# Ten projection tiles of the second block by seven products in place of eight

## The reference, cut to what matters

```python
h = rms_norm_2(x, g_pre) * (1 + scale) + shift
proj = h @ w_in                    # 1024 x 1024 by 1024 x 9216
q, k, v, g_att, u, g_lru, merge = jnp.split(proj, split_at, axis=-1)
y_a = (dilated_attention(q, k, v) * jax.nn.silu(g_att)) @ w_pa
u = causal_depthwise_conv(u, conv_w, conv_b)
y_b = (rg_lru(u, w_rg, b_rg, w_ig, b_ig, lru_lambda) * jax.nn.silu(g_lru)) @ w_pb
gate_a, gate_b = jnp.split(jax.nn.sigmoid(merge), N_BRANCHES, axis=-1)
out = (gate_a * y_a + gate_b * y_b) @ w_o
return x + gate * rms_norm_2(out, g_post)
```

## Time and profile before

| | us | share of span | instructions |
| --- | --- | --- | --- |
| median of the runs | 2834.89 | | |
| span of the profiled execution | 2834.6 | | 33566 |
| TensorE matmul (PE) | 2789.5 | 98% | 13780 |
| TensorE weight load (PEld) | 2343.3 | 83% | 13780 |
| VectorE (DVE) | 1838.1 | 65% | 2069 |
| ScalarE (ACT) | 1514.1 | 53% | 1619 |
| GpSimd (POOL) | 136.6 | 5% | 81 |

### The profile page before, as it was taken

The page is one execution under the profiler, slowest core; times in us unless marked ns, Lnnn a source line. Parts: engine busy times, 40 slices in busy tenths (PEclk is TensorE's granted clock), DMA queues, the critical chain, the costliest instruction groups (busy, mean ns, idle before and its releaser), DMA issues.

```text
span 2834.6 us, 33566 instructions
## 1 busy us (share of the span) xinstructions
PE 2789.5 (98%) x13780; PEld 2343.3 (83%) x13780; DVE 1838.1 (65%) x2069; ACT 1514.1 (53%) x1619; POOL 136.6 (5%) x81
## 2 busy tenths in 40 slices
PE   8999999879999999999999999999999999999999
PEld 7889988768888888888888878888888888888887
DVE  7564467778888888888888886333332256544344
ACT  5322322247777777777777776333333389743022
POOL 0211000110000000000000000000000011100000
PEclk9999999989999999999999999999999999999999
DMA  6222157789999999999999951110112211343332
GB/s 200 89 74 78 72 178 264 267 331 383 386 386 386 382 386 382 388 384 386 390 383 387 377 210 75 60 60 25 59 60 60 69 48 63 99 158 131 112 134 89
DMA packets 137273, 598.97 MB, mean 211 GB/s; under 512 B 17952, under 2 KB 39840, under 8 KB 80672
## 3 DMA queue, kind: packets, MB, share of 16 engines
q1 hardware_dynamic: 132224, 580.10, 54.7%
q0 software_dynamic: 4464, 16.25, 2.2%
q10 hardware_dynamic: 432, 0.47, 0.1%
HBM read 543.06 MB, written 52.53 MB: 210 GB/s over the span
## 4 chain that ended last, share of the span: by engine, by line
PE 97%; DVE 2%; ACT 0%; issue 0%; DMA 0%; SPq 0%; DVEq 0%; ACTq 0%
PE bank L442 26%; PE bank L444 25%; PE bank L443 25%; PE bank L1871 12%; PE bank L450 3%; PE bank L459 1%; PE bank L2444 1%; PE bank L1420 1%; PE bank L778 1%; PE bank L2817 0%; DVE r_sc L1654 0%; DVE r_at L1655 0%; DVE r_best L1651 0%; PE bank L2445 0%; PE bank L838 0%
## 5 line engine op out<-in xcount | busy, mean ns | idle before, releaser
L1819 DVE TENSOR_TENSOR e_wl<-e_raw,e_wh 128x2048 fp32r<-128x2048 f32 x381 | 870.8, 2291 | 123.9 <-ACT e_wh L1811 123.4
L1811 ACT ACTIVATE e_wh<-e_raw 128x2048 fp32r<-128x2048 f32 x384 | 735.6, 1919 | 184.6 <-PE bank L444 100.9
L442 PE MATMUL bank<-b_hid_h,b_wh 128*128 128x512 f32 x1148 | 452.1, 394 | 0.2
L444 PE MATMUL bank<-b_hid_h,b_wl 128*128 128x512 f32 x1148 | 447.4, 390 | 0.0
L443 PE MATMUL bank<-b_hid_l,b_wh 128*128 128x512 f32 x1148 | 446.9, 389 | 0.0
L442 PE MATMUL bank<-e_wh,e_xh 128*128 128x512 f32 x1020 | 403.4, 395 | 0.0
L444 PE MATMUL bank<-e_wh,e_xl 128*128 128x512 f32 x1020 | 398.1, 390 | 0.0
L443 PE MATMUL bank<-e_wl,e_xh 128*128 128x512 f32 x1020 | 396.9, 389 | 0.0
L442 PEld LDWEIGHTS bank<-b_hid_h,b_wh 128*128 128x128 f32 x1148 | 215.6, 188 | 46.5 <-issue 2.9
L444 PEld LDWEIGHTS bank<-b_hid_h,b_wl 128*128 128x128 f32 x1148 | 215.5, 188 | 45.6
L443 PEld LDWEIGHTS bank<-b_hid_l,b_wh 128*128 128x128 f32 x1148 | 215.7, 188 | 42.8
(11 more groups left out here) (508 smaller groups left out, 4354.8 us busy)
## 6 DMA issues: line engine op xcount, KB each, us to landing
e_raw<-in_e_gate_dram SPq DMA_DIRECT2D x128, 1024.0 KB, 7.4
e_raw<-in_e_up_dram SPq DMA_DIRECT2D x128, 1024.0 KB, 7.6
e_raw<-in_e_down_dram SPq DMA_DIRECT2D x128, 1024.0 KB, 7.7
b_raw<-in_w_dram SPq DMA_DIRECT2D x36, 1024.0 KB, 6.0
a_raw<-in_w_dram SPq DMA_DIRECT2D x12, 1024.0 KB, 5.6
a_mod_w<-in_w_mod_dram SPq DMA_DIRECT2D x48, 256.0 KB, 4.7
a_x<-in_x_dram SPq DMA_DIRECT2D x16, 512.0 KB, 5.5
scr_sig<-a_sig SPq DMA_DIRECT2D x32, 256.0 KB, 2.3
```

Of the source, the lines that this page charges most:

```text
L442: e.matmul(out, a[0], b[0], start=first, stop=False)
L444: return e.matmul(out, a[1], b[0], start=False, stop=last)
L1811: e.activation(t.e_wh[s][:, 0:2048], t.e_raw[slot][:, 0:2048], ACT.Copy).then_inc(*e.inc("e_round", i))
L1819: e.tensor_tensor(t.e_wl[s][:, 0:2048], t.e_raw[slot][:, 0:2048], t.e_wh[s][:, 0:2048].bitcast(F32), ALU.subtract).then_inc(*e.inc("e_spli ...
```

## The change

**Seven products.** Ten of the 36 tiles are computed by Strassen's identity: a weight tile is cut in four quarters (2 x 512 inputs, 2 x 128 channels), the input `b_hid` likewise (2 x 512 inputs, 2 x 512 tokens), and seven products of quarters or of sums of quarters replace eight (`pe_set`). A set has 7 products of 4 steps of three matmuls. The ten sets stand ahead of attention, the six of merge gates first, then four of values (`SET_KINDS`). The sums of weight quarters are made by GpSimd, four to a set (`pool_set_sums`), each of the seven parts is rounded and split for itself, VectorE adds the products out of the banks (`dve_set`, seven operations a set), and SyncE stores the results to DRAM, from where values come back ahead of their head (`load_values`).

**Crossed inputs.** The seven products need four differences of quarters of the unrounded input. So the turn keeps its shifted pieces in `b_c`, one for each half, which lies where `b_t` 0 to 7 lay, and each half's turn waits for four of the stores of `b_t`. GpSimd makes two of the four differences, VectorE two, in four steps each, in place; ScalarE rounds them (`mix_cols`), VectorE makes their low parts.

**Order.** The values of heads 0 to 3 (tiles 0 and 1, the old way) run while the halves are turned, in place of head 0's queries and keys; ScalarE evicts them through `early`. Attention holds only queries and keys and gates between its steps. Behind the recurrence 8 merge units are left in place of 32; the mixes stand two units apart at 2i+5 (turned at 2i+7), 6 of them behind the merges among the units of branch b, which now run as 16 units of 8 steps, with 16 units of branch a (4 steps) behind them. The recurrence's output is split in tiles: 0 and 1 at slot 5, 2 to 7 at place 8. `w_o` is rounded between branch a's units, and the first output tile is computed with 512 columns.

```diff
         self.b_t = [sb(f"b_t{i}", y + 4096 + 1024 * i, [128, 1024]) for i in range(8)]
-        self.b_tmp = [sb(f"b_tmp{i}", z + at, [128, 512]) for i, at in enumerate((5120, 5632, 8192))]
+        self.b_c = [sb(f"b_c{half}", y + 4096 + 4096 * half, [128, 8, 512]) for half in range(2)]
+        places = {1: (12288, 14336), 3: (16384, 18432), 2: (20480, 0), 4: (2048, 4096)}
+        self.mix_cols = {n: tuple(sb(f"b_m{n}{part}", y + at, [128, 4, 512], F32R) for part, at in zip("hl", ats))
+                         for n, ats in places.items()}
+        self.part_w = [(sb(f"b_ph{i}", spl + 1024 * i, [128, 4, 128], F32R),
+                        sb(f"b_pl{i}", spl + 1024 * i + 512, [128, 4, 128], F32R)) for i in range(8)]
+        self.set_sum = [sb(f"b_sum{i}", y + 8192 + 512 * i, [128, 4, 128]) for i in range(4)]
+        self.set_y = [[sb(f"b_sy{i}{s}", y + (6144, 10240)[s] + 512 * i, [128, 512]) for s in range(2)]
+                      for i in range(4)]
+        self.v_y = [sb(f"b_vy{i}", raw + 2048 + 512 * i, [128, 512]) for i in range(4)]
+        self.scr_v = self.dram("scr_v", [12, 128, 1024])
...
 def act_turn_second(e, t, half, behind):
...
+    e.wait_ge(*e.at(f"b_t_out{half}", 4 * half + 3))
...
-            tmp_free(e, half, kk)
-            e.activation(t.b_tmp[kk % 3][:, :], t.bank[b][:, :], ACT.Identity, scale=t.scale2[:, kk:kk + 1],
+            e.activation(t.b_c[half][:, kk, :], t.bank[b][:, :], ACT.Identity, scale=t.scale2[:, kk:kk + 1],
...
+def pool_cross(e, t, n, j):
+    first, second = t.b_c
+    if n == 1:
+        e.wait_ge(*e.at("b_hid", 0, j))
+        e.wait_ge(*e.at("b_shifted", 1, j))
+        e.tensor_tensor(first[:, j, :], second[:, j, :], first[:, j, :],
+                        ALU.subtract).then_inc(*e.inc("crossed_pool", n, j))
+    else:
+        e.wait_ge(*e.at("b_hid", 0, 4 + j))
+        e.wait_ge(*e.at("crossed", 2, j))
+        e.tensor_tensor(first[:, 4 + j, :], first[:, 4 + j, :], second[:, 4 + j, :],
+                        ALU.subtract).then_inc(*e.inc("crossed_pool", n, j))
...
+def dve_cross(e, t, j):
...
+    e.wait_ge(*e.at("b_shifted", 1, 4 + j))
+    e.tensor_tensor(second[:, j, :], second[:, 4 + j, :], second[:, j, :],
+                    ALU.subtract).then_inc(*e.inc("crossed", 3, j))
+    e.wait_ge(*e.at("b_hid", 1, 4 + j))
+    then(e).tensor_tensor(second[:, 4 + j, :], second[:, 4 + j, :], first[:, j, :],
+                          ALU.subtract).then_inc(*e.inc("crossed", 2, j))
...
+SET_KINDS = [("merge", i) for i in range(6)] + [("values", 2 + i) for i in range(4)]
+SUM_OF = {3: 0, 1: 1, 2: 2, 5: 3}
...
+def sp_load_set(e, t, g):
+    s = g % 2
+    if g == 0:
+        e.wait_ge(*e.at("w_split", 0))
+    elif g == 1:
+        e.wait_ge(*e.at("w_split", 1))
+        for n in range(4):
+            for half in range(2):
+                e.wait_ge(*e.at(f"v_out{n}", n, half))
+    else:
+        e.wait_ge(*e.at("part_low", 7 * (g - 2) + 6))
+    e.dma_start(t.b_raw[s][:, 0:2048], t.ins["w2_sets"][g]).then_inc(*e.dma(f"raw{s}_in", "set", g))
...
+def pool_set_sums(e, t, g):
...
+    e.wait_ge(*e.at(f"raw{g % 2}_in", "set", g))
+    for k, (i, x, y, how) in enumerate(((3, a[1][0], a[1][1], ALU.add), (1, s[0], a[0][0], ALU.subtract),
+                                        (2, a[0][0], a[1][0], ALU.subtract), (5, a[0][1], s[1], ALU.subtract))):
...
+def pe_set(e, t, g):
+    rows = lambda k, half: [a[:, 4 * k:4 * k + 4, 512 * half:512 * half + 512] for a in t.b_hid]
+    cross = lambda n: [a[:, :, :] for a in t.mix_cols[n]]
+    for i, x in enumerate((rows(0, 0), cross(2), cross(3), cross(1), rows(1, 0), rows(1, 1), cross(4))):
+        q, b = 7 * g + i, set_bank(g, i)
+        if g == 0 and i in (1, 2, 3, 6):
+            e.wait_ge(*e.at("crossed_low", {1: 2, 2: 3, 3: 1, 6: 4}[i]))
+        e.wait_ge(*e.at("part_low", q))
+        e.wait_ge(*e.free(b))
+        for kk in range(4):
+            m = three(e, t.bank[b][:, :], [a[:, kk, :] for a in t.part_w[q % 8]], [a[:, kk, :] for a in x],
+                      kk == 0, kk == 3)
+        m.then_inc(*e.fill(b, "set_full", g, i))
+        e.mark("part_spent", q)
...
     squares(0, 1, 2, 3)
     act_scale_root(e, t, 0)
     act_scale(e, t, 0)
     act_turn_second(e, t, 0, behind_first)
     squares(5)
+    early(0, 0)
+    early(1, 0)
+    squares(6)
+    act_square_rows(e, t, 7, 1)
+    act_scale_root(e, t, 1)
+    act_scale(e, t, 1)
+    early(2, 0)
+    early(3, 0)
+    act_turn_second(e, t, 1, lambda kk: None)
+    e.activation(t.stat[:, 3, :], t.stat[:, 2, :], ACT.Sqrt).then_inc(*e.inc("r1_root"))
+    act_round_crossed(e, t, 1)
+    act_round_crossed(e, t, 3)
+    act_round_crossed(e, t, 2)
+    early(0, 1)
+    early(1, 1)
+    act_round_crossed(e, t, 4)
+    for q in range(4):
+        act_round_part(e, t, q)
+    early(2, 1)
+    early(3, 1)
+    for q in range(4, AHEAD):
+        act_round_part(e, t, q)
+    for q in range(N_PARTS):
+        act_round_part(e, t, q + AHEAD)
+        if q == N_PARTS - 2:
+            act_round_w(e, t, HEAD_TILE)
...
+def dve_set(e, t, g, i):
...
+    if i == 1:
+        e.wait_ge(*e.at("set_one", g))
+        set_out_free(e, g, 5)
+        e.tensor_tensor(second, bank, first, ALU.add).then_inc(*e.evict(b, "set_taken", g, 1))
...
+    if i == 3:
+        e.wait_ge(*e.at("set_taken", g, 2))
+        set_out_free(e, g, 3)
+        e.tensor_tensor(fourth, bank, third, ALU.add).then_inc(*e.inc("set_taken", g, 3))
+        if kind == "values":
+            e.mark("set_made", g, 3)
+        e.tensor_tensor(second, bank, second, ALU.add).then_inc(*e.evict(b, "set_fourth", g))
...
+    for j in range(4):
+        dve_cross(e, t, j)
+    for n in (1, 3, 2):
+        dve_low_crossed(e, t, n)
+    for q in range(2):
+        dve_low_part(e, t, q)
+    dve_low_crossed(e, t, 4)
+    for q in range(2, AHEAD):
+        dve_low_part(e, t, q)
...
+def pool_second(e, t):
+    for j in range(4):
+        pool_cross(e, t, 1, j)
+    for j in range(4):
+        pool_cross(e, t, 4, j)
+    for g in range(N_SETS):
+        pool_set_sums(e, t, g)
...
 def sp_second(e, t):
+    sp_load_set(e, t, 0)
     sp_store_t(e, t)
...
+    for half in range(2):
+        for n in range(4):
+            early(n, half)
+    sp_load_set(e, t, 1)
+    for q in range(N_PARTS):
+        g, i = divmod(q, 7)
+        if i == 0 and g + 2 < N_SETS + 2 and g:
+            if g + 1 < N_SETS:
+                sp_load_set(e, t, g + 1)
+            else:
+                sp_load_w(e, t, HEAD_TILE)
+        sp_set(e, t, g, i)
...
+N_MERGES = 8
+MIXES = {2 * i + 5: i for i in range(8)}
+MIX_TURNS = {2 * i + 7: i for i in range(8)}
...
+def act_round_lru(e, t, kk):
+    e.wait_ge(*e.at("lru_made", 7))
+    if kk < 2:
+        e.wait_ge(*e.at("w_split", MERGE_TILE))
+    else:
+        e.wait_ge(*e.at("merge", N_MERGES - 1))
...
+        if n == 0:
+            e.wait_ge(*e.free(1))
+            for kk in range(8):
+                for other in range(2):
+                    m = products(other, (kk,), 7, wt, None)
...
+        elif n > 1:
+            products(n, range(8), 7, wt, None).then_inc(*e.fill(n % 4, "up2", n))
...
+    for n in range(16):
+        i = 8 + n // 4
...
+        e.wait_ge(*e.at("m_ba", 3 + 4 * (n % 2)))
+        products(n, range(4), 3, wt, t.m_ba).then_inc(*e.fill(n % 4, "up2", 16 + n))
```

More of the change, by code:

```diff
@@ L2206, in pe_place, with sets_stored @@
+def sets_stored(e):
+    for g in (N_SETS - 2, N_SETS - 1):
+        for k in range(4):
+            e.wait_ge(*e.at(f"set_out{2 * k + g % 2}", g))
 def pe_place(e, t, i, part):
@@ L2747, in sp_second @@
         tile, first, last = unit_tile(u)
-        if u == ("qk", 0, 1, 0):
-            sp_load_w(e, t, 2)
-        if first and tile:
+        if first:
             sp_load_w(e, t, tile + 2)
@@ L2877, in pe_lru @@
                     pe_lru_gates(e, t, ct - 1)
-    mixes, turns = mix_slots()
-    for slot in range(32):
-        ct, which, half, b = slot // 4, slot // 2 % 2, slot % 2, slot % 4
-        tile = 28 + ct
+    for slot in range(N_MERGES):
+        which, half, b = slot // 2 % 2, slot % 2, slot % 4
+        tile = MERGE_TILE + slot // 4
         e.wait_ge(*e.at("w_split", tile))
@@ L2889, in pe_lru @@
             pe_lru_gates(e, t, 7)
[L2890 to L2895 removed]
+        if slot in MIX_TURNS:
+            pe_mix_turn(e, t, MIX_TURNS[slot])
 def act_lru(e, t):
@@ L2932, in act_lru @@
         e.activation(t.l_wgs[0][:, :], t.l_wg[s][:, :], ACT.Copy).then_inc(*e.inc("wg_high", ct))
-    mixes, turns = mix_slots()
-    for slot in range(32):
-        n, ct = slot % 4, slot // 4
-        if slot % 4 == 0 and ct < 7:
-            act_round_w(e, t, 28 + ct + 1)
+    for slot in range(N_MERGES):
+        n = slot % 4
+        if slot == 0:
+            act_round_w(e, t, MERGE_TILE + 1)
+        act_mix_steps(e, t, slot)
         e.wait_ge(*e.at("merge", slot))
@@ L3062, in sp_lru @@
     for ct in range(8):
-        sp_load_w(e, t, 20 + ct + 2)
```

(43 more changed lines are left out.)

707 lines of the change are left out of this document (429 added, 278 removed).

## The result

The changed kernel takes 2858.02 us (median of 4 runs, 2853.84 to 2858.23), the kernel before beside it 2834.87. The ratio is 1.0078, 95% interval 1.0064 to 1.0092: 23 us slower, where 13 were forecast with the same sign. The profiled execution has a span of 2856.2 us.

The account below looks back on a forecast made before the run. TensorE, busy 2789.5 of 2834.6 us, was taken as the bound. Terms -28.0 + 9.9 + 2.8 + 3.3 + 8.1 + 14.1 + 2.8 + 1.2 = +14.2 gave 2849.1, stated as 2848 us; range 2818 to 2862.

Parts of the forecast that it names:

- saved: Fewer matmuls in ten projection tiles, a cheaper first output tile and a few attention waits gone: 28.0 us less.
- Step 1: Start of second block: the first turn waits for four b_t stores queued behind the first set's load; 9.9 us.
- 2, clock behind it: After the first turn's idle stretch TensorE runs at half clock; 2.8 us, 0 to 3.1.
- Step 3: Second turn starts late, as ScalarE first evicts values 2 and 3; 3.3 us, no half clock with it.
- Step 4: First product: VectorE just fits alone, but GpSimd takes turns with it; 5.3 us stall plus 2.8 of clock, 8.1.
- Step 5: The ten sets run at TensorE's pace, 19.1 us each, loads landing 11 us before use; nothing, up to 5 us.
- Step 6: Mixes behind the recurrence: the branch b input's rounding stands behind mix 1 and turn 0; 14.1 us plus 2.8 clock.
- 7, the end: The last unit has 12 matmuls, 2.7 us, too short for the 3.7 us of work beside it; 1.2 us.
- Rival A: Faster: ScalarE and VectorE have low halves ready when TensorE asks, behind the turn and slot 7; 2826 us, chance 0.20.
- Rival D: VectorE bounds the sets, as sums keep it off longer: some 2 us a set, 2868 us, chance 0.07.

Follow-up runs that it names:

- e1: Against the changed kernel, SyncE stores b_t 0 to 3 before it issues the load of the first set, not behind it; 2841.71 us.
- e10: Against the changed kernel, b_t 0 to 3 are stored ahead of the first set's load, but only after weight tile 0's low half; one execution, 2849.3 us.
- e2: Against the changed kernel, ScalarE evicts values 2 and 3 of the first half behind the second turn, not ahead of it; 2850.18 us.
- e5: Against the changed kernel, VectorE, not GpSimd, makes the fourth crossed input (four operations between low halves of the first and second part); 2854.70 us.
- e9: Against the changed kernel, fourth cross on VectorE, values evicted behind part 0's rounding, low halves of parts 1 to 3 between the crosses; 2851.19 us.
- e4: Against the changed kernel, the load of set g+2 is issued at the start of set g, not behind the stores one set later; 2851.93 us.
- e3: Against the changed kernel, mixes and their turns one slot later, and the split of the recurrence's output ahead of a weight piece; 2841.67 us.
- e6: Against the changed kernel, VectorE's low half of the last merge weight tile waits for GpSimd's two low parts of the last gates; 2854.41 us.

## Why the prediction was right, and where it was short

The sign and the mechanism were right: the products save what was worked out, and the order around them costs more. The forecast added 42.2 us to the saving, the traces show 50.6.

| step | forecast | measured | shown by |
| --- | --- | --- | --- |
| saved | 28.0 | 28.2 | balance |
| 1, first turn | 9.9 | 12.1 | e1, e10 |
| 2, clock behind it | 2.8 | 3.1 | windows |
| 3, second turn | 3.3 | 3.4 + 3.1 | e2 |
| 4, first product | 5.3 + 2.8 | 3.6 + 3.0 | e5, e9 |
| 5, the sets | 0 | 2.7 | e4 |
| 6, the mixes | 14.1 + 2.8 | 12.5 + 2.9 | e3 |
| 7, the end | 1.2 | 1.1 | waits |
| last gates | not seen | 2.2 + 1.7 | e6, e5, e9 |

Where a cell has two numbers, the second is the half clock. The rows are of the one profiled execution of the kernel after; the clock differs in others.

*Step 1* had the mechanism and too fast a transfer. I took the 355 GB/s of a window in which the queue was full (the last line of the earlier trace rows, not rows 5 as the prediction has it). The load and four stores, 3.15 MB, took from 1702.3 to 1713.8, 11.5 us: 274 GB/s.

*Step 3* failed in one clause: that a wait of 3.3 us brings no half clock because one row showed 1.00 through the first 4.4 us of an idle stretch. That is one idle stretch, and no rule for shorter ones: in the kernel after, waits of 3.4, 3.6 and 2.2 us had the half clock behind them. At the second turn this was worth 3.1 (1.7 in five other runs, nothing in e10), and 1.7 at the gates.

*Step 4* had the right cause. Until the first product VectorE lost 4.9 us beside GpSimd (three crosses 1.6 for 0.69, a low half 3.38 for 2.28, another 1.74 for 0.69), near the 5 to 7 counted. e5 gave back the crosses and the first low half, 3.8 us, and the wait went. TensorE waited 3.6 only: VectorE had 1.3 us of slack where I had said that it just fits. The prediction has the half clock hide "the smaller waits of the next two products"; one of them, the bank in e5, was not small.

*Step 5* is the step that was wrong in kind. It counted the load as issued "about 2 us into set g". It was issued only when SyncE had sent the four results of set g-1: 7.7 us into set 2, and 1.6 to 1.7 us later in each of the next three. The range (up to 5) held it, the value 0 did not. The same step left no margin for GpSimd's sums (1.3, 1.6, 1.3 and 1.7 us where 1.1 to 1.2 had been read), but e4 shows that these cost TensorE nothing.

*Step 6*, the largest, came about as worked out, 1.6 us shorter. In the kernel after mix 0 ends at 2611.1, the heads of mix 1 land at 2615.77, and the tiles of the split follow behind mix 1 and turn 0:

```profile
2615.77 0.17 DVE L3363 TENSOR_REDUCE m_small<-m_a 128x4 f32<-128x12 f32 x1 [3.52 <-DMA m_a<-scr_heads]
...
2624.56 5.78 ACT L3454 ACTIVATE p_lh<-l_out 128x1024 fp32r<-128x1024 f32 x6
```

*The last gates* were not touched by the change, and I did not look there. Before, GpSimd began 0.2 us ahead of VectorE's `l_out`, which held `l_out` for 3.30 us, so VectorE's low half of the merge tile began only at 2440.3, when GpSimd's second operation had 0.4 us left. Now VectorE begins first, its low half starts 1.55 us behind GpSimd's first operation, and the two meet. What moved GpSimd's start stays open (e6).

Rival A (the narrow engines keep up) was wrong as the kernel stands: items 4 and 6 came to 22.0 us, where it asked for less than 5.1. Its against-argument, two loads in a row that no slack shortens, holds for the mixes, but not for TensorE: e3 put the split in front of them. With another order, and four operations moved from GpSimd to VectorE, the two engines do keep up, and the time is 2809.6. Rival D (VectorE bounds the sets) is refuted by e4.

## What to carry to other kernels

Where one engine has all the time, work out the saving from its pace, and then go through every in-order queue for what now stands ahead of the first thing that the engine needs; here a handful of such places, mended by moving lines and by giving four operations to another engine, turned 23 us of loss into 25 of gain. To each new wait of TensorE of 2 us or more add up to 3 us for a half clock behind it (the shortest that had one here is 1.98 us, in e10). A wait that is taken away can uncover one that lay hidden behind it, so look at the next products as well. What stands ahead of a transfer on the engine that issues it, and in its queue, is a dependency of that transfer.
